# Hybrid attention block: the input norm is applied after the first projections instead of before them

## The reference

```
h    = rmsnorm(x, g_pre_mix)                 # x * rsqrt(mean(x*x) + 1e-6) * g
proj = h @ w_in[l]     # sparse q,k,v | indexer q (8 heads x 64), indexer k (64), head weights (8) | stick-breaking q,k,v | gates
score[t,s] = sum_h relu(qi[t,h] . ki[s] * 64**-0.5) * wi[t,h] * 8**-0.5     # the indexer; top 128 keys per token are kept
o_a  = attention over the kept keys, with a relative-position bias
o_b  = stick-breaking attention
x    = x + rmsnorm((sigmoid(gate_a) * (o_a @ W_a) + sigmoid(gate_b) * (o_b @ W_b)) @ W_out)
x    = x + rmsnorm(swiglu(rmsnorm(x)) @ W_down)
```

## Time and profile before

| | us |
|---|---|
| median of 3 runs | 799.68 (796.98 to 803.74) |
| the profiled execution | 797.15 |
| its span | 795.4 |
| PE busy | 779.8 (98%) |
| DVE, ACT, POOL busy | 379.0, 346.9, 421.1 |

### The profile page before, as it was taken

One profiled execution on the slowest core, in us unless ns is written; L12 is line 12 of the kernel. 1 busy time (PEld: TensorE's weight loads), 2 busy tenths in 40 slices (PEclk: granted clock), 3 DMA queues, 4 the chain that ended last, 5 costly groups with the idle time before them and its releaser, 6 DMA issues.

```text
span 795.4 us, 10525 instructions
## 1 busy us (share of the span) xinstructions
PE 779.8 (98%) x3758; PEld 653.5 (82%) x3758; DVE 379.0 (48%) x524; ACT 346.9 (44%) x508; POOL 421.1 (53%) x244
## 2 busy tenths in 40 slices
PE   6999999999999999999999999999999999999996
PEld 4887888888888888888888988888888888888885
DVE  4359989989656565379337100000000020544564
ACT  5474166766758585643255222222222232233242
POOL 5278455766777878334563244444443443443463
PEclk9999999999999999999999999999999999999998
DMA  7211452311304231222293113332233332222312
GB/s 240 92 54 54 128 169 69 99 54 54 104 10 119 68 110 56 79 81 106 77 320 106 54 54 105 105 105 88 73 103 105 105 105 84 77 104 105 105 53 106
DMA packets 103771, 77.30 MB, mean 97 GB/s; under 512 B 3633, under 2 KB 95801, under 8 KB 103738
## 3 DMA queue, kind: packets, MB, share of 16 engines
q1 hardware_dynamic: 103738, 76.87, 30.9%
HBM read 74.75 MB, written 3.68 MB: 99 GB/s over the span
## 4 chain that ended last, share of the span: by engine, by line
PE 90%; POOL 3%; DMA 2%; DVE 2%; ACT 1%; issue 0%; SPq 0%; POOLq 0%; ACTq 0%; DVEq 0%
PE ps L453 22%; PE ps L425 20%; PE ps L426 20%; PE ps L427 20%; PE ps L640 2%; PE ps L629 2%; POOL f_bias L1127 2%; PE ps L608 1%; PE ps L610 1%; DMA raw<-in_w_gate_up 1%; POOL w_lo L1075 1%; DMA raw<-in_w_in 1%; DMA raw<-in_w_out 1%; DVE h_lo L1236 0%; ACT y_buf L779 0%
## 5 line engine op out<-in xcount | busy, mean ns | idle before, releaser
L1075 POOL TENSOR_TENSOR w_lo<-raw,w_hi 128x1024 fp32r<-128x1024 f32 x86 | 207.7, 2415 | 287.4 <-ACT w_hi L750 258.6
L425 PE MATMUL ps<-h_hi,w_hi 128*128 128x512 f32 (+1 forms) x656 | 251.7, 384 | 1.9 <-DVE h_lo L1236 1.9
L427 PE MATMUL ps<-h_hi,w_lo 128*128 128x512 f32 (+1 forms) x656 | 249.1, 380 | 0.0
L426 PE MATMUL ps<-h_lo,w_hi 128*128 128x512 f32 (+1 forms) x656 | 248.8, 379 | 0.0
L750 ACT ACTIVATE w_hi<-raw 128x1024 fp32r<-128x1024 f32 (+1 forms) x81 | 85.9, 1060 | 309.3 <-PE ps L427 204.4
L425 PEld LDWEIGHTS ps<-h_hi,w_hi 128*128 128x128 f32 x656 | 123.5, 188 | 24.0 <-ACT w_hi L750 1.8
L427 PEld LDWEIGHTS ps<-h_hi,w_lo 128*128 128x128 f32 x656 | 123.3, 188 | 23.6
L426 PEld LDWEIGHTS ps<-h_lo,w_hi 128*128 128x128 f32 x656 | 123.6, 188 | 21.4
L1494 DVE TENSOR_TENSOR act<-silu,ps 128x512 f32 (+1 forms) x22 | 15.1, 687 | 211.3 <-PE ps L427 211.3
L1148 POOL TENSOR_TENSOR w_lo<-raw,w_hi 128x1024 fp32r<-128x1024 f32 x30 | 77.3, 2581 | 31.8 <-ACT w_hi L864 31.4
L1499 DVE TENSOR_TENSOR d_lo<-act,d_hi 128x512 fp32r<-128x512 f32 x18 | 43.1, 2396 | 51.7 <-ACT d_hi L1017 51.7
(11 more groups left out here) (183 smaller groups left out, 1253.4 us busy)
## 6 DMA issues: line engine op xcount, KB each, us to landing
raw<-in_w_in SPq DMA_DIRECT2D x44, 512.0 KB, 4.1
raw<-in_w_gate_up SPq DMA_DIRECT2D x44, 512.0 KB, 4.5
raw<-in_w_down SPq DMA_DIRECT2D x22, 512.0 KB, 3.9
raw<-in_w_out SPq DMA_DIRECT2D x8, 512.0 KB, 3.8
x_in<-in_x SPq DMA_DIRECT2D x4, 512.0 KB, 5.4
raw<-in_w_branch_sb SPq DMA_DIRECT2D x8, 256.0 KB, 2.9
raw<-in_w_branch_sparse SPq DMA_DIRECT2D x8, 256.0 KB, 3.0
x<-in_x SPq DMA_DIRECT2D x4, 512.0 KB, 7.8
```

The source lines that it names most:

```text
L425: mm(acc, whi_c, a_hi_, start=first, stop=False)
L426: mm(acc, whi_c, a_lo_, start=False, stop=False)
L427: return mm(acc, wlo_c, a_hi_, start=False, stop=last)
L1075: nc.gpsimd.tensor_tensor(w_lo[:, at(u), :], raw[:, at((d % 2) * 2 + u), :], w_hi[:, at(u), :], sub).then_inc(w_lo_done, 1)
```

## The change

The host hands over a second copy of x, transposed and packed by chunks: `in_first` holds per chunk 128 channels by 972 columns, which are the 512 tokens, 456 columns of weights (query tiles 0 to 2 and `kw`), the gain of the channel and padding. SP loads it as `xf`, eight DMAs of 486 KB.

The first pass of PE (L512) goes chunk by chunk over these 456 columns, 12 matmuls each, on x times gain without the token's factor. Beside it ACT squares the chunks, DVE adds the squares up, and two matmuls with ones (L521, L522) sum them over the partitions at chunk 4, so that the inverse root `rstd_all` comes as 128x512. Then x in `xf` is scaled by `rstd_all`, even chunks on DVE, odd ones on POOL, and split again in `h_hi` and `h_lo` (ACT L823, DVE L1305) for query tile 3 and everything after. The keys are multiplied by `rstd_all` as they leave PSUM (`ki_f`), the head weights by `rstd_all` or, for the six heads of the first three tiles, by its square (`w_scale`). The transposes of x and the multiplication of the gain by a row of ones are gone; 14 transposes of `ident` on itself (`WARM`) stand at PE's start. The scores of the indexer now begin when all four query tiles are split, and 6, 4, 4 and 2 chunk steps of the T_QKB tiles stand ahead of its four pairs of heads. The masks' constants and the zeros of `qi_lo` are made later on POOL. `T_QI3` and what follows have tile numbers two lower.

```diff
+QI_FIRST = 3
+WQ = QI_FIRST * P + KW
+XW = S + WQ
+FIRST = XW + 4
+WARM = 14
...
-T_QI = 0
-T_QKB = T_QI + PAIRS
+T_QI3 = 1
+T_QKB = T_QI3 + 1
...
+        for c in range(KC):
+            sp.dma_start(xf[:, c, 0:FIRST], first[c, :, :]).then_inc(first_in[c], 16)
-        for t in range(2):
-            sp.dma_start(x_in[:, t, :], x_rows[:, t, :]).then_inc(x_in_got[t], 16)
...
+        pe.sem_inc(tile_done, 1)
         pe.wait_ge(const, 2)
+        for _ in range(WARM):
+            nc.tensor.transpose(bank(6)[:, 0:P], ident[:, :], ident[:, :])
+
+        first_accs = [(bank(j), j * P, (j + 1) * P) for j in range(QI_FIRST)] + [(ps[0:KW, 4, :], QI_FIRST * P, WQ)]
+
+        def first_pass(w, act, c, first, last):
+            for acc, a, b in first_accs:
+                ins = mm(acc, w[:, c, a:b], act[:, c, :], start=first, stop=last)
+            return ins
+
+        for c in range(KC):
+            pe.wait_ge(xg_hi_done, c + 1)
+            pe.wait_ge(*((wq_hi_done, c) if c else (wq_hi0_done, 1)))
+            first_pass(wq_hi, h_hi, c, c == 0, False)
+            if c == KC // 2:
+                pe.wait_ge(sum_lo_done, 1)
+                mm(bank(5), ones[:, :], sum_hi[:, :], start=True, stop=False)
+                mm(bank(5), ones[:, :], sum_lo[:, :], start=False, stop=True).then_inc(sum_spread, 1)
+            pe.wait_ge(xg_lo_done, c + 1)
+            first_pass(wq_hi, h_lo, c, False, False)
+            pe.wait_ge(wq_lo_done, c + 1)
+            first_pass(wq_lo, h_hi, c, False, c == KC - 1).then_inc(chunk_done, 1)
...
-        for t in range(3):
-            turn(0, t, x_in)
-        first_part(0, T_QI, 0, 0, 2)
-        turn(0, 3, x_in)
-        first_part(0, T_QI, 1, 0, 2)
-        first_part(0, T_QI, 0, 2, 4)
-        first_part(0, T_QI, 1, 2, 4)
...
+        weights(T_QI3)
         for c in range(KC):
+            pe.wait_ge(xn_lo_done, c + 1)
+            ins = proj_part(bank(3), T_QI3 % 2, c, c + 1)
+        ins.then_inc(tile_done, 1)
+
+        pe.wait_ge(wi_kept, 1)
...
+            if h == 0:
+                pe.wait_ge(qi_lo_done, PAIRS)
+                pe.wait_ge(ki_halves_done, 3)
+                pe.wait_ge(w_tok_done, 1)
+                pe.wait_ge(small_kept, 1)
...
+        def heads_b_steps(first, end):
+
+            for s in range(first, end):
+                u, c = s // KC, s % KC
+                if c == 0:
                     weights(T_QKB + u)
+                    pe.wait_ge(qi_lo_done, u + 1)
+                ins = proj_part(bank(u), u, c, c + 1)
+                if c == KC - 1:
+                    ins.then_inc(tile_done, 1)
+
+        steps = (0, 6, 10, 14, 16)
+        for j in range(PAIRS):
+            heads_b_steps(steps[j], steps[j + 1])
+            indexer_scores(2 * j)
+            indexer_scores(2 * j + 1)
...
+        def round_x(c):
+            sc.wait_ge(first_in[c], 16)
+            run(h_hi[:, c, :], xf[:, c, 0:S], ACT.Copy, scale=xf[:, c, XW:XW + 1]).then_inc(xg_hi_done, 1)
+
+        def round_wq(c):
+            run(wq_hi[:, c, 0:WQ], xf[:, c, S:XW], ACT.Copy).then_inc(wq_hi_done, 1)
+
+        def square_x(c):
+            sc.wait_ge(first_in[c], 16)
+            if c >= 2:
+                sc.wait_ge(squares_added, max(1, c - 2))
+            run(sq[:, c % 2, :], xf[:, c, 0:S], ACT.Square).then_inc(x_squared, 1)
+
+        def round_scaled(c):
+            sc.wait_ge(*((x_scaled_gp, c // 2 + 1) if c % 2 else (x_scaled, c // 2 + 1)))
+            sc.wait_ge(chunk_done, c + 1)
+            run(h_hi[:, c, :], xf[:, c, 0:S], ACT.Copy, scale=xf[:, c, XW:XW + 1]).then_inc(xn_hi_done, 1)
...
+        round_x(0)
+        for c in range(1, KC // 2 + 1):
+            round_x(c)
+            round_wq(c)
+            square_x(2 * c - 2)
+            square_x(2 * c - 1)
+        sc.wait_ge(squares_added, KC - 1)
+        run(sum_hi[:, :], sq_sum[:, :], ACT.Copy).then_inc(sum_hi_done, 1)
+        for c in range(KC // 2 + 1, KC):
+            round_x(c)
+            round_wq(c)
+        sc.wait_ge(var_spread, 1)
+        run(std_all[:, :], var_all[:, :], ACT.Sqrt).then_inc(std_spread, 1)
+        split(T_QI3 // 2, T_QI3 % 2)
+        for c in range(KC):
+            round_scaled(c)
+            if c == 4:
+                split(T_QKB // 2, 0)
...
+            if t == 1:
+                sc.wait_ge(ki_scaled, 1)
+                run(ki_hi[0:HD, :], ki_f[0:HD, :], ACT.Copy).then_inc(ki_hi_done, 1)
+            if t < QI_FIRST:
+                sc.wait_ge(chunk_done, KC)
+            else:
+                split(T_QKB // 2, 1)
+                sc.wait_ge(tile_done, T_QI3 + 1)
...
+        def rest_wq(c):
+            gp.wait_ge(*((wq_hi_done, c) if c else (wq_hi0_done, 1)))
+            nc.gpsimd.tensor_tensor(wq_lo[:, c, 0:WQ], xf[:, c, S:XW], wq_hi[:, c, 0:WQ], sub).then_inc(wq_lo_done, 1)
+
+        def scale_x(c):
+            gp.wait_ge(xg_lo_done, c + 1)
+            nc.gpsimd.tensor_tensor(xf[:, c, 0:S], xf[:, c, 0:S], rstd_all[:, :], ALU.mult).then_inc(x_scaled_gp, 1)
+
+        gp.sem_inc(w_lo_done, 1)
+        for c in range(KC):
+            rest_wq(c)
+            if c == 3:
+                gp.wait_ge(wq_lo_done, c + 1)
+                for h in range(2):
+                    if h:
+                        gp.wait_ge(qi_lo_zeroed, h)
+                    nc.gpsimd.memset(qi_lo[HD - HD * h:P - HD * h, h::2, :].bitcast(F32), 0.0).then_inc(qi_lo_zeroed, 1)
+                gp.wait_ge(qi_lo_zeroed, 2)
+        gp.wait_ge(rstd_spread, 1)
+        for c in (1, 3, 5):
+            scale_x(c)
+            if c == 3:
+                split(T_QI3 // 2, T_QI3 % 2)
+        scale_x(7)
+        split(T_QKB // 2, 0)
+        gp.wait_ge(w_lo_done, T_QKB + 1)
+        nc.gpsimd.memset(zeros8[:, :], 0.0).then_inc(const_gp, 1)
...
+        def rest_x(c):
+            ve.wait_ge(xg_hi_done, c + 1)
+            stt(h_lo[:, c, :], xf[:, c, 0:S], xf[:, c, XW:XW + 1], h_hi[:, c, :], ALU.mult, sub).then_inc(xg_lo_done, 1)
+
+        def add_squares(c):
+            ve.wait_ge(x_squared, c + 1)
+            if c == 1:
+                tt(sq_sum[:, :], sq[:, 0, :], sq[:, 1, :], ALU.add).then_inc(squares_added, 1)
+            else:
+                ve.wait_ge(squares_added, c - 1)
+                tt(sq_sum[:, :], sq_sum[:, :], sq[:, c % 2, :], ALU.add).then_inc(squares_added, 1)
+
+        def scale_x(c):
+            ve.wait_ge(xg_lo_done, c + 1)
+            tt(xf[:, c, 0:S], xf[:, c, 0:S], rstd_all[:, :], ALU.mult).then_inc(x_scaled, 1)
+
+        def rest_scaled(c):
+            ve.wait_ge(xn_hi_done, c + 1)
+            stt(h_lo[:, c, :], xf[:, c, 0:S], xf[:, c, XW:XW + 1], h_hi[:, c, :], ALU.mult, sub).then_inc(xn_lo_done, 1)
...
+        ve.wait_ge(first_in[0], 16)
+        nc.vector.tensor_copy(wq_hi[:, 0, 0:WQ], xf[:, 0, S:XW]).then_inc(wq_hi0_done, 1)
+        rest_x(0)
+        for c in range(1, KC // 2 + 1):
+            rest_x(c)
+            if c > 1:
+                add_squares(2 * c - 2)
+            add_squares(2 * c - 1)
+        ve.wait_ge(sum_hi_done, 1)
+        tt(sum_lo[:, :], sq_sum[:, :], sum_hi[:, :], sub).then_inc(sum_lo_done, 1)
+        rest_x(KC // 2 + 1)
+        ve.wait_ge(sum_spread, 1)
+        ts(var_all[:, :], bank(5), 1.0 / D, EPS, ALU.mult, ALU.add).then_inc(var_spread, 1)
+        for c in range(KC // 2 + 2, KC):
+            rest_x(c)
+        ve.wait_ge(std_spread, 1)
+        nc.vector.reciprocal(rstd_all[:, :], std_all[:, :]).then_inc(rstd_spread, 1)
+        ve.wait_ge(rstd_spread, 1)
+        for c in range(0, KC, 2):
+            scale_x(c)
+            if c >= 2:
+                rest_scaled(c - 2)
+                rest_scaled(c - 1)
+        nc.vector.tensor_copy(w_scale[HD:KW, :], rstd_all[HD:KW, :]).then_inc(scale_kept, 1)
+        ve.wait_ge(scale_kept, 1)
+        plain = HD + 2 * QI_FIRST
+        tt(w_scale[HD:plain, :], rstd_all[HD:plain, :], rstd_all[HD:plain, :], ALU.mult).then_inc(scale_squared, 1)
+        rest_scaled(KC - 2)
+        rest_scaled(KC - 1)
+        ve.wait_ge(chunk_done, KC)
+        tt(ki_f[0:HD, :], ps[0:HD, 4, :], rstd_all[0:HD, :], ALU.mult).then_inc(ki_scaled, 1)
+        ve.wait_ge(scale_squared, 1)
+        stt(wi_t[HD:KW, :], ps[HD:KW, 4, :], float(HEADS) ** -0.5, w_scale[HD:KW, :], ALU.mult, ALU.mult).then_inc(wi_kept, 1)
...
+    w, d = inputs["w_in"][0], KC * P
+    laid = np.concatenate([inputs["x"][0].T, w[:, COL_QI:COL_QI + QI_FIRST * P], w[:, COL_KI:COL_KI + KW],
+                           inputs["g_pre_mix"][0][:, None], np.zeros((d, FIRST - XW - 1), np.float32)], axis=1)
+    arrays["in_first"] = np.ascontiguousarray(laid.reshape(KC, P, FIRST))
```

More of the change, by code:

```diff
@@ L176, in build @@
     top[0] = zone2
-    x_in = sb("x_in", [TB, D])
+    sq = sb("sq", [2, S])
+    sq_sum = sb("sq_sum", S)
+    sum_hi, sum_lo = sb("sum_hi", S, F32R), sb("sum_lo", S, F32R)
+    rstd_all, ki_f, wi_t = sb("rstd_all", S), sb("ki_f", S), sb("wi_t", S)
     qi_twice, qi_lo = sb("qi_twice", [HEADS, S], F32R), sb("qi_lo", [HEADS, S], F32R)
```

(1 more changed line is left out.)

187 lines of the change are left out of this document (55 added, 132 removed).

## The result

The changed kernel takes 814.46 us (median; 810.29 to 816.41) against 800.51 for the kernel before on the same chip: 1.0168 times, 95% interval 1.0108 to 1.0228. It is slower, and the median lies above my range (791 to 811). The profiled execution took 815.29, its span is 813.6: 18.2 more than the 795.4 of before.

The account below looks back on a forecast made before the run. PE bounds the kernel: its end is its start plus its work. Value tiles starting at 71.9, not 66.96, add 4.9 to 797.15: 802.1 profiled; the median 2.5 above is 804.6, taken as 803, range 791 to 811.

Parts of the forecast that it names:

- The start: PE's first pass begins at 5.0 instead of 15.39; taken alone worth 10.4 us, and the transposes 0.9.
- From the chunks to the inverse root: Squares, sums and root: the inverse starts at about 23.2, takes 1.7, and `rstd_all` is ready at 24.9.
- Inverse to scaled keys: DVE and POOL take turns on SBUF between `rstd_all` and `ki_f`: 18.9 us, scaled keys at 43.8.
- Rival 1: DVE and POOL collisions matter less between inverse and keys, so keys come before 38.9; 789 to 798 us, chance 0.24.
- Keys to first score: ACT's `ki_hi`, query tile copies and a split, then DVE's `qi_lo`: 10.7 us, first score at 54.5.
- The guard behind C: DVE's top-k scan, which waited 2.65 for ACT: a score summed up to 2.6 later costs nothing.
- C: Start of the value tiles, the first value matmul: forecast 71.9 against 66.96 before, 4.9 later.
- First score to value tiles: Chunk steps 6.8, heads 8.3 and last relus 1.8, sum 16.9, plus 0.5 for colliding additions.
- moving `f_bias` would not help: On POOL before the value tiles: no gain from moving it, since both ways there end together, at 71.4 and 70.6.
- POOL's way to the value tiles: Second T_QKB split ends at 53.0 on POOL, and the value tiles follow 17.64 later, at 70.6.
- Behind 66.96 the program is the same, 728.4 us to the end: From the first value matmul to the end of the span nothing changes: 728.4 us.
- rival 2: Slow inverse, DVE held off over several POOL operations, slow matmuls behind PE's idle time; 806 to 812 us, chance 0.20.

Follow-up runs that it names:

- no_gp_scaling: Changed kernel without POOL's four scalings of the odd chunks, which stay unscaled; its one execution took 810.44 us.
- filler: Changed kernel with thirty transposes of the identity in PE's idle piece ahead of the value tiles; 811.07 us, 1.0113 times the kernel before.
- steps_late: Changed kernel with `f_bias` ahead of the second T_QKB split on POOL and PE's chunk steps moved behind the heads they delay; 806.5 us, 1.008 times the kernel before.
- mid_hold: Changed kernel with two more waits on POOL in the last norm; 809.97 us, 1.0125 times the kernel before.
- no_scaling: Changed kernel without the second pass over x (scaling, rounding, second `h_lo`); 801.84 us, 0.9996 times the kernel before.
- combo: Changed kernel with the edits of steps_late and mid_hold together; 804.11 us, 1.0053 times the kernel before.

## Why the prediction was wrong

**The start** (pass at 5.0; it was 4.86) was right. **From the chunks to the inverse root** the end was right by luck: `rstd_all` was ready at 25.4 for 24.9, because two errors cancel. The inverse began at 22.04 for 23.2, and it took 3.34 for 1.7. The upper bound of 2.7, from 5 ns a column between two small forms, was no bound: it is (3.34 - 0.16)/511 = 6.2 ns a column.
**Inverse to scaled keys**, the stretch on which I had said all hung, was right in mechanism and size: 18.35 against 18.9, and no_gp_scaling shows that it is the turns with POOL. Rival 1 is thereby refuted. **Keys to first score** took 10.9 against 10.7. PE's idle 4 to 5 us in front of the score came out as 1.2 only because PE ran the steps ahead of it at a granted clock of 0.50; in filler, with 1.00 there, it was 4.0, and the first score came at 54.84. The guard behind C held, too: from the last `h_lo` to the first `m_hi` it is 269.2 before and after.

**First score to value tiles** is the first step that failed: "I add 0.5 for additions of scores that collide with `f_bias` and `w_lo` and hold up relus (0 to 3)". The additions were held up 4.1 and, at 71.50, 2.0, and PE waited 5.8 for relus, where I had 2.3 in all (the 1.8 of the last relus and this 0.5). I had the row for it, 6.86 in the earlier trace rows, and read it as something the program covers. It was covered by the half tile behind the last heads, and I had myself written that this cover is gone. PE's own work was not the error: without those waits it is 16.1 in the changed kernel, and 16.1 in steps_late, where the same work in another order hides them. With this falls "moving `f_bias` would not help", which is worth 1.9. Its reason failed as well: POOL's way to the value tiles, forecast to end at 70.6, ended at 66.4, 10 ahead of C. `f_bias` mattered by what it held up on DVE and not by its own end.

**"Behind 66.96 the program is the same, 728.4 us to the end"** is the second. The same instructions took 737.0. Of the 8.6 more, 2.5 are the clock behind PE's idle piece. I gave it to rival 2 and placed it at the scores; in the changed kernel it came at the value tiles. The other 6.1 are the coin of the last norm. No view of one profile could show it, but the range of the three runs could hint at it: 797 to 804, with my profile at its lower end.

Together these are the miss of the profiled time, 815.29 for 802.1: 4.7 of C, 2.5 and 6.1. The sum also gave 804.6 for the median, and I wrote 803 without a reason.

Rival 2 (C = 76 to 80, 806 to 812, 0.20) was the case that came in C = 76.6 and the slow matmuls; the time lies above its 812 by the coin. Of its parts, the inverse was slow (3.34, not 4), but the keys were not 3 to 5 later: DVE was held off over several POOL operations at the additions of scores instead. Like for like, both kernels with a good throw of the coin, the change costs 12.1 (9.6 and 2.5), a span of 807.5. This is a sum and not a run; the nearest run is mid_hold, whose norm takes 1.0 more than 289.0, with 808.3.

The gain went in this order. The 10 us of PE at the start were given back in query tile 3 (forecast). The second pass over x costs 12.1 of C (no_scaling), and the 2.5 that would be left without it go into the clock.

## What to carry to other kernels

Before counting a gain at the start, find the engine whose chain reaches the next fixed point: here it is DVE, in turns with POOL, and work taken from PE but put on these two is paid in full. When a change removes the work that covered a wait, price that wait at the longest row it has in the trace, not at the average, and look for an order of the same work that covers it again. When the profiled execution lies at the edge of the runs' range, part of its time may be luck; profile the kernel again before comparing.

## What the hardware showed that I had not expected

A DVE operation with both operands in SBUF doesn't always wait for POOL. At 62.09 DVE stood 4.83 through seven POOL operations in a row, the first of which had begun at 62.04. At 58.5 it was the other way: DVE's two additions took their usual time, and POOL's 8x1 operations, 0.27 to 0.30 where DVE is idle, took 0.87 on average. DVE, then POOL, in the changed kernel:

```profile
58.49 1.28 DVE L1377 SCALAR_TENSOR_TENSOR score<-relu_buf,w_tok,score 128x512 f32<-128x512 f32 x2
```

```profile
58.50 1.73 POOL L1174 TENSOR_SCALAR f_bias<-zeros,rel_t 8x1 f32<-8x1 f32 x2
```

With the starts at `y_buf` above, whichever of the two began first went on in every one of these cases. Why DVE did not get in between the seven operations at 62.09, no run here shows.

The slow level of the tensor clock can fall where it costs nothing: from 40 to 50 in the changed kernel it was 0.50 to 0.59, and filler, with 1.00 from 40 to 54, has its first score no earlier. Or it falls on the first scores, at 0.56 to 0.59 from 54 to 62 in combo, and C is 2 us later than in steps_late, the same program up to there.
